# Rotary rows by DMA, and compressed blocks read with a stride

## The reference, cut to what matters

```
def partial_rope(x, pos):            # 16 of the 64 channels of each head are rotated
    ang = pos[:, None] * inv_freq    # 8 frequencies
    x1, x2 = x[..., :8], x[..., 8:16]
    rot = concat([x1 * cos - x2 * sin, x2 * cos + x1 * sin])
    return concat([rot, x[..., 16:]])

q_n   = partial_rope(q_b) ...        # 8 query heads of 64
k_cmp, k_slc, k_win = partial_rope(kc_b), partial_rope(ks_b), partial_rope(kw_b)

def compress_blocks(kv, pos_emb, w1, w2):       # kv: 256 tokens, 2 groups of 64 channels
    idx = arange(15)[:, None] * 16 + arange(32) # 15 overlapping blocks of 32 tokens
    blocks = kv[:, idx] + pos_emb[:, None, :]
    hid = silu(einsum('bnlgd,ldh->bgnh', blocks, w1))
    return einsum('bgnh,hd->bgnd', hid, w2)
```

## Time and profile before

| | |
|---|---|
| median of the runs | 890.04 us |
| profiled execution, its own time | 890.07 us |
| its span | 888.3 us |
| PE busy | 874.8 us (98%) |
| DVE busy | 586.1 us (66%) |
| ACT busy | 440.2 us (50%) |
| POOL busy | 51.3 us (6%) |
| DMA queue of SP | 150.44 MB |

### The profile page before, as it was taken

How to read it: one execution, slowest core, us unless ns; L and a number is a source line. 1 busy time by engine, 2 the same in 40 slices (tenths; PEclk the granted TensorE clock), 3 DMA queues, 4 the chain that set the end, 5 groups by cost and what they waited for, 6 DMA issues and landing times.

```text
span 888.3 us, 13795 instructions
## 1 busy us (share of the span) xinstructions
PE 874.8 (98%) x5624; PEld 759.6 (86%) x5624; DVE 586.1 (66%) x898; ACT 440.2 (50%) x644; POOL 51.3 (6%) x78
## 2 busy tenths in 40 slices
PE   8999999999999999999999999999999999999997
PEld 6888999898999888888889999877788888888885
DVE  5785664565656755555686997956477667777544
ACT  6644444753345544544485652466254555555442
POOL 1000000000020110000020015200000100000000
PEclk9999999999999999999999999999999999999999
DMA  9757644456454554556757683412555556665441
GB/s 294 239 190 227 223 144 142 143 166 183 127 184 153 184 179 153 175 183 198 263 145 248 159 174 95 144 49 49 143 190 181 180 184 190 189 190 190 166 166 48
DMA packets 127813, 151.67 MB, mean 171 GB/s; under 512 B 16983, under 2 KB 93142, under 8 KB 127750
## 3 DMA queue, kind: packets, MB, share of 16 engines
q1 hardware_dynamic: 127466, 150.44, 53.8%
q10 hardware_dynamic: 220, 0.28, 0.1%
q0 software_dynamic: 64, 0.07, 0.0%
HBM read 148.67 MB, written 3.68 MB: 172 GB/s over the span
## 4 chain that ended last, share of the span: by engine, by line
PE 87%; DVE 8%; ACT 2%; issue 1%; DMA 1%; POOL 0%; POOLq 0%; SPq 0%; ACTq 0%; DVEq 0%
PE bank L519 18%; PE bank L521 17%; PE bank L520 17%; PE bank L1357 9%; PE bank L546 5%; PE bank L1360 5%; PE bank L548 2%; DVE w_lo L2141 2%; DVE arena L2553 1%; PE bank L1017 1%; PE bank L751 1%; PE bank L731 1%; PE bank L850 1%; DMA arena<-in_x 1%; PE bank L711 0%
## 5 line engine op out<-in xcount | busy, mean ns | idle before, releaser
L2141 DVE TENSOR_TENSOR w_lo<-ring,w_hi 128x2048 fp32r<-128x2048 f32 (+1 forms) x134 | 297.5, 2230 | 120.4 <-ACT w_hi L1566 120.0
L1566 ACT ACTIVATE w_hi<-ring 128x2048 fp32r<-128x2048 f32 (+1 forms) x134 | 249.1, 1861 | 93.0 <-PE bank L521 71.5
L519 PE MATMUL bank<-h_both,w_hi 128*128 128x256 f32 x488 | 140.3, 287 | 0.4 <-DVE w_lo L2141 0.4
L520 PE MATMUL bank<-h_both,w_hi 128*128 128x256 f32 x488 | 138.0, 283 | 0.0
L521 PE MATMUL bank<-h_both,w_lo 128*128 128x256 f32 x488 | 138.0, 283 | 0.0
L1357 PE MATMUL bank<-h_both,w_hi 128*128 128x512 f32 x352 | 96.5, 395 | 0.8 <-DVE arena L2867 0.8
L519 PEld LDWEIGHTS bank<-h_both,w_hi 128*128 128x128 f32 x488 | 93.5, 192 | 2.4 <-issue 1.4
L520 PEld LDWEIGHTS bank<-h_both,w_hi 128*128 128x128 f32 x488 | 93.6, 192 | 0.1
L521 PEld LDWEIGHTS bank<-h_both,w_lo 128*128 128x128 f32 x488 | 93.5, 192 | 0.0
L519 PE MATMUL bank<-w_hi,h_both 128*128 128x512 f32 (+1 forms) x192 | 73.7, 384 | 0.0
L521 PE MATMUL bank<-w_hi,h_both 128*128 128x512 f32 (+1 forms) x192 | 71.5, 372 | 0.0
(11 more groups left out here) (387 smaller groups left out, 1525.9 us busy)
## 6 DMA issues: line engine op xcount, KB each, us to landing
ring<-in_w_in SPq DMA_DIRECT2D x59, 1024.0 KB, 5.1
ring<-in_w_gate_up SPq DMA_DIRECT2D x44, 512.0 KB, 4.7
ring<-in_w_down SPq DMA_DIRECT2D x10, 1024.0 KB, 5.0
ring<-in_w_mem_kv SPq DMA_DIRECT2D x8, 1024.0 KB, 10.0
ring<-in_w_gla_out SPq DMA_DIRECT2D x4, 1024.0 KB, 5.0
ring<-in_w_x_out SPq DMA_DIRECT2D x4, 1024.0 KB, 5.2
ring<-in_w_dsa_out SPq DMA_DIRECT2D x4, 1024.0 KB, 5.2
ring<-in_w_o SPq DMA_DIRECT2D x4, 1024.0 KB, 4.9
```

What stands on the lines that cost most here:

```text
L519: mm(o, ah, bh, start=start, stop=False, skip_group_check=True)
L520: mm(o, ah, bl, start=False, stop=False, skip_group_check=True)
L1566: act(w_hi[:, k % NHI, at:m], ring[:, order.index(name) % NSLOT, at:m], ACT.Copy)\
L2141: tt_(w_lo[:, i, at:m], ring[:, i, at:m], w_hi[:, k % NHI, at:m].bitcast(F), ALU.subtract)\
```

## The change

SP now moves the rotary rows. For each of the seven tiles 0, 1, 2 and 4 to 7, six DMAs inside the core's own memory collect the 16 rotary rows of both groups in a compact tile `rot` and once more, with the halves swapped, in `rot_turned` (`gather`, 42 DMAs). DVE does the rotation there with three instructions for each of two compact tiles (`rope`), the sign being in the table of sines. SP writes the rows back (`spread`, 14 DMAs). For the blocks of compressed tokens SP copies kc and vc into `blocks` (`block_rows`, 24 DMAs, of which 8 need the rotated rows); POOL writes the position rows beside them once; the 64 matmuls read their stationary operand with a stride of 16 tokens, and one matmul with a constant `pick` adds the partial rows and the position part. On PE the banks r0 to r3, sh0 and sh1 are gone, on POOL `rope_cos`, on DVE the sine products, the additions and the sixteen block additions. In the first block one small matmul (bank ik2) becomes a copy on ACT. SP's list of weight loads is not changed, but the DMAs stand in it:

```
             for i, name in enumerate(order):
                 s = i % NSLOT
+                if name == order[order.index("nq0") + NSLOT + 1]:
+                    sp.wait_ge(signal("roped"), 1)
+                    block_rows(0, 0, 16, lambda g: rot[16 * g:16 * g + 16, 0, :], "kc_blocks")
+                    spread(0)
                 if i >= NSLOT:
                     sp.wait_ge(*unit_used[order[i - NSLOT]])
+                    before = order[i - NSLOT]
+                    if before in ("kcks", "kwvc", "nq0", "nq1"):
+                        sp.wait_ge(*read(before))
+                    if before == "kcks":
+                        gather(0)
+                        gather(1)
+                        block_rows(0, 16, 64, lambda g: ns[64 * g + 16:64 * g + 64, 0, :], "kc_blocks")
+                    if before == "kwvc":
+                        gather(2)
+                        block_rows(1, 0, 64, lambda g: ns[64 * g:64 * g + 64, 3, :], "vc_blocks")
+                    if before == "nq0":
+                        gather(4)
+                        gather(5)
+                    if before == "nq1":
+                        gather(6)
+                        gather(7)
+                    if before == "vsvw":
+                        sp.wait_ge(signal("roped"), 2)
+                        spread(1)
```

```
+            def gather(tile):
+                i = int(tile > 4)
+                for g in range(2):
+                    at = 32 * rot_tiles[i].index(tile) + 16 * g
+                    sp.dma_start(rot[at:at + 16, i, :], ns[64 * g:64 * g + 16, tile, :]).then_inc(signal(f"gathered{i}"), 16)
+                    sp.dma_start(rot_turned[at:at + 8, i, :], ns[64 * g + 8:64 * g + 16, tile, :])\
+                      .then_inc(signal(f"gathered{i}"), 16)
+                    sp.dma_start(rot_turned[at + 8:at + 16, i, :], ns[64 * g:64 * g + 8, tile, :])\
+                      .then_inc(signal(f"gathered{i}"), 16)
+            def spread(i):
+                for a, tile in enumerate(rot_tiles[i]):
+                    for g in range(2):
+                        at = 32 * a + 16 * g
+                        sp.dma_start(ns[64 * g:64 * g + 16, tile, :], rot[at:at + 16, i, :])\
+                          .then_inc(signal(f"spread{i}"), 16)
+            def block_rows(kv, a, b, source, done):
+                for part, g, q in itertools.product(range(2), range(2), range(2)):
...
+                    sp.dma_start(blocks[kv][part][64 * q + a:64 * q + b, 256 * g:256 * g + n], source(g)[:, at:at + n])\
+                      .then_inc(signal(done), 16)
```

On PE:

```
             head_products("qg", 0)
-            pe.wait_ge(*read("kwvc"))
-            rope_turn("r0", 0, 2)
-            rope_turn("r1", 2, 1)
             project_channels("nq1", h_parts)
             head_transposes("kk", 4)
-            pe.wait_ge(*read("nq0"))
-            rope_turn("r2", 4, 2)
             pe.wait_ge(signal("silu_done"), 6)
             head_transposes("vt", 8)
-            pe.wait_ge(*read("nq1"))
-            rope_turn("r3", 6, 2)
-            pe.wait_ge(signal("rope_done"), 1)
-            for kv, tile in ((0, 0), (1, 3)):
-                bank = open_bank(f"sh{kv}")
...
             project_tokens("vsvw", h_parts)
             w = (plain_unit("w1k"), plain_unit("w1v"))
             bank = open_bank("hid")
-            for kv in range(2):
-                pe.wait_ge(*read(f"sh{kv}"))
+            pe.wait_ge(signal("positions"), 4)
+            pe.wait_ge(signal("vc_blocks"), 16 * 8)
+            pe.wait_ge(signal("kc_blocks"), 16 * 16)
...
-            pe.wait_ge(signal("rope_done"), 4)
+            pe.wait_ge(signal("spread0"), 16 * 8)
             level(1)
             hidden_sum()
             nsa_logits(0)
             nsa_logits(1)
             compressed_keys()
             level_end(1)
+            pe.wait_ge(signal("spread1"), 16 * 6)
             compressed_scores()
```

On DVE, whose scores also wait for both spreads, because they overwrite `rot`:

```
+            def rope(i):
+                n = rot_rows[i]
+                x, turned = rot[0:n, i, :], rot_turned[0:n, i, :]
+                ve.wait_ge(signal(f"gathered{i}"), 16 * 6 * len(rot_tiles[i]))
+                tt_(turned, turned, const("sin")[0:n, :], ALU.mult)
+                step(tt_(x, x, const("cos")[0:n, :], ALU.mult))
+                tt_(x, x, turned, ALU.add).then_inc(signal("roped"), 1)
...
-            lows(splits_by["r1"] + 1)
+            rope(0)
+            lows(splits_by["qg1"] + 1)
...
+            lows(ahead[0])
+            rope(1)
             ahead[0] = splits.index("z1") + 1
...
+            ve.wait_ge(signal("spread0"), 16 * 8)
+            ve.wait_ge(signal("spread1"), 16 * 6)
             for i in range(4):
                 nsa_scores(i)
```

More of the change, by code:

```diff
@@ L56, in _const_columns @@
     for name, width in (("ident", 128), ("diag3", 384), ("keep", S), ("chunk", 128), ("bucket", 383), ("pad", 1),
-                        ("lev", 6 * 64), ("id64", 64), ("chunk64", 64), ("after", 128), ("rope", 128), ("cos", S), ("sin", S), ("selg", 256),
-                        ("ones", 1),
+                        ("lev", 6 * 64), ("id64", 64), ("chunk64", 64), ("after", 128), ("cos", S), ("sin", S),
+                        ("pick", 64), ("ones", 1),
                         ("cneg", 2 * 16), ("cvis", 2 * 16)):
@@ L95, in shape_constants @@
     put("diag3", np.concatenate([diag, np.zeros((128, 128)), diag], 1))
-    rot = np.zeros((128, 128), np.float32)
-    cos = np.ones((128, S), np.float32)
-    sin = np.zeros((128, S), np.float32)
     freq = np.float32(500000.0) ** (-np.arange(8, dtype=np.float32) / np.float32(8))
     ang = (np.arange(S, dtype=np.float32)[:, None] * freq.astype(np.float32)[None, :]).astype(np.float32)
[L101 to L116, removed]
+    sign = np.where(np.arange(128) % 16 < 8, -1.0, 1.0).astype(np.float32)
+    put("cos", np.cos(ang).T[np.arange(128) % 8])
+    put("sin", np.sin(ang).T[np.arange(128) % 8] * sign[:, None])
+    pick = np.zeros((128, 64), np.float32)
+    for q in range(4):
+        for n in range(30):
+            pick[32 * q + n + n // 15, 30 * (q // 2) + n] = 1
+            pick[32 * q + 15, 30 * (q // 2) + n] = 1
+    put("pick", pick)
     put("ones", np.ones((128, 1)))
@@ L326, in build @@
         cblk_at = raw_at + 8 * S
-        cblk = [flat(cblk_at + 480 * i, 480).rearrange("p (j n) -> p j n", j=16) for i in range(2)]
+        blocks = [[flat(mb_at + 1024 * kv + 512 * part, 512) for part in range(2)] for kv in range(2)]
+        rot, rot_turned = tiled(prob_at, 2, S), tiled(prob_at + 512, 2, S)
+        rot_tiles, rot_rows = ((0, 1, 2, 4), (5, 6, 7)), (128, 96)
         hid, hid_rows = flat(cblk_at + 968, 64), flat(cblk_at, 128)
@@ L1058, in _ @@
                     kv, k = q // 2, j + q % 2
-                    ins = mm(bank[32 * q:32 * q + 32, 0:128], flat(cblk_at + 480 * kv + 30 * k, 32), w[kv][:, k, :],
+                    by_offset = blocks[kv][k // 8].rearrange("p (m s) -> p s m", s=16)
+                    ins = mm(bank[32 * q:32 * q + 32, 0:128], by_offset[:, 2 * (k % 8), :], w[kv][:, k, :],
                              start=j == 0, stop=j == 14, tile_position=(0, 32 * q), skip_group_check=True)
@@ L1066, in hidden_sum @@
                 bank = open_bank("hs")
-                by_branch = ident.rearrange("p (a b) -> p a b", a=2)
-                mm(bank[:, 0:60], hid_rows, by_branch[:, :, 0:30], start=True, stop=False)
-                done("hs", mm(bank[:, 0:60], hid_rows, by_branch[:, :, 32:62], start=False, stop=True))
+                done("hs", mm(bank[:, 0:60], hid_rows, const("pick")[:, 0:60], start=True, stop=True))
             z_weights = {}
@@ new lines, in spread @@
+            def spread(i):
[6 more added lines that the diff above has]
+                for part, g, q in itertools.product(range(2), range(2), range(2)):
+                    n = 240 if g == 0 or part == 1 else 256 - q
+                    if part == 1:
+                        n -= q
+                    at = 16 * part + q
+                    sp.dma_start(blocks[kv][part][64 * q + a:64 * q + b, 256 * g:256 * g + n], source(g)[:, at:at + n])\
+                      .then_inc(signal(done), 16)
@@ L1630, in _ @@
             sc.wait_ge(*full("small"))
+            act(ikT[0], bank_of("small")[64:128, 0:256], ACT.Copy)
             act(smallT, bank_of("small")[:, 0:256], ACT.Copy).then_inc(bank_reader("small"), 1)
@@ L2078, in _ @@
             nc.gpsimd.tensor_tensor(egc, egc, cv[:, 0:4, :], ALU.mult).then_inc(signal("q_decayed"), 1)
+            for kv in range(2):
+                for part in range(2):
+                    lots = blocks[kv][part].rearrange("p (m s) -> p m s", s=32)[:, 7 + 8 * (1 - part)::8, 16:32:2] \
+                        if part == 1 else blocks[kv][part][:, 240:256:2].unsqueeze(1)
+                    pos = cmp_pos[kv][:, 8 * part:8 * part + 8].unsqueeze(1).broadcast_to([128, 1 + part, 8])
+                    nc.gpsimd.tensor_copy(lots, pos).then_inc(signal("positions"), 1)
             gp.wait_ge(*read("ss"))
```

(9 more changed lines are left out.)

32 lines of the change are left out of this document (1 added, 31 removed).

## The result

The changed kernel takes 915.43 us (914.92 to 916.83, 6 runs) against 890.03 (889.73 to 890.46, 6 runs) of the kernel before: a ratio of 1.0286, 95% interval 1.0275 to 1.0296. It is slower, as forecast, but by 25.4 us and not by 4.9, and outside the range. The profiled execution took 914.92 us with a span of 913.1, 24.8 longer than before.

The account below looks back on a forecast made before the run. PE, busy 874.8 of 888.3 us, was taken as the bound, with SP's queue as second limit. Terms 4.6 - 0.3 - 0.4 + 1.0 = +4.9 on 890.07 gave 895.0 us, range 889 to 901.5.

Parts of the forecast that it names:

- What it puts into SP's queue: SP's weight loads: 74 small DMAs ahead of z1 at 0.41 us per issue delay z1, so hs starts 4.6 us later.
- Rotations and copies off PE, 4.9 us, and hid earlier: PE before hid: removing rotations and copies takes about 4.9 us off PE's path, so hid is reached at 551.
- rival 1: SP's queue: small copies cost much less than 0.3 us, z1 is issued as before, hs 5.0 us earlier: 884.4 us; chance 0.14.
- The other new waits end earlier: Waits for block rows and spreads: rotated block rows land at 549.4, spreads at 552.7 and near 563.7, before they are needed.
- hs released by ACT behind z1, with PE idle for 8 to 10 us: Sign in the profile after: PE idles 8 to 10 us in front of hs until ACT copies hid near 564.
- One matmul for hs and the lower clock, -0.3 and +1.0: PE from hs on: one matmul instead of two saves 0.3 us; the lower clock after idling costs 1.0 (0 to 5.75).
- rival 3: PE behind hs: lower clock holds the whole stretch, +5.75 instead of +1.0, 899.7 us; with longer issues 904; chance 0.15.
- The copy on ACT in place of a matmul in the first block, -0.4: First block: a PE matmul of 0.64 us becomes a copy on ACT, saving 0.4 us (0 to 0.6).

Follow-up runs that it names:

- experiment 1: Kernel before, with groups of eight small copies issued behind its end: SP took 0.63 us per copy inside the core, 0.45 with an end in device memory.
- experiment 5: Changed kernel with each SP weight load issued ahead of its slot's copies and z1 ahead of the gathers of nq0: 914.03 us, ratio 1.027.
- experiments 6 to 8: Changed kernel, its 80 copies divided over SP, POOL and ACT: loads first 895.31 us; then z0 and the next load held 892.64; then queue order mended, z0 unheld 890.6.

## Why the prediction was wrong

**The step that failed** is the issue term of "What it puts into SP's queue": "I take 0.41, the mean of the two with 16 rows, and keep 0.36 and 0.46". The queue took 0.68 per copy in the changed kernel, and experiment 1 has 0.63 on an idle chip. 74 x (0.68 - 0.41) = 20 us, and that is the miss: z1 left at 574.46 instead of the predicted 555.3, 19.2 us later. From there the working holds. z1 landed after 5.5 us (5.9 predicted), ACT split it and copied hid, and hs followed: +23.07 instead of +4.6.

The error under it was one of kind. The rows taken as neighbours all have one end in device memory, and experiment 1 gives 0.45 for those, too, so they had been read rightly. They were no bound for a copy with both ends in the core. The sentence in front of the number said that the trace has no such copy, but the interval was then made from the spread inside the other kind, 0.36 to 0.46, as if that covered the unknown. With 74 repeats each tenth of a microsecond is 7.4 us; the range ended 6.5 us above the forecast and could not hold an error of 0.27.

**The other terms.**
- Rotations and copies off PE, 4.9 us, and hid earlier: right in size. Without copies hid starts at 550.40 (551 predicted) and hs 6.1 earlier; rival 1 had 884.4 for that, and 884.06 was measured. So what it said PE would gain was right; its price for an issue (under 0.3) was off by more than the forecast's.
- "The other new waits end earlier": wrong, by the same term. PE waited 11.84 us in front of hid for the block copies. This cost nothing on top, because hs waited for z1 anyway; experiment 5 shows that it takes over the moment z1 is early.
- hs released by ACT behind z1, with PE idle for 8 to 10 us: right in kind, but it was 13.96.
- One matmul for hs and the lower clock, -0.3 and +1.0: together +1.8 measured, from hs to the compressed scores 5.56 us instead of 3.72. Windows of the profile after (the eighth figure is the granted clock):

```profile
575.00:580.00 5.00, 0.00 (x0) 0.00 (x0) 1.18 (x3) 0.00 (x0) 0.00 (x0) 0.50 0.74 221
580.00:586.00 6.00, 3.39 (x18) 2.54 (x18) 3.37 (x9) 3.33 (x6) 0.00 (x0) 0.50 0.72 242
586.00:588.00 2.00, 2.00 (x40) 1.68 (x40) 1.39 (x10) 0.94 (x5) 0.00 (x0) 0.68 1.05 391
588.00:592.00 4.00, 4.00 (x80) 3.58 (x74) 3.46 (x15) 3.26 (x15) 0.13 (x1) 1.00 0.67 244
```

  PE stood idle, the clock fell to its 1.2 GHz level, and the matmuls behind hs ran at it until about 587: the logits took 2.93 us instead of 1.58. The value taken near the lower end of 0 to 5.75 was about a microsecond too small; rival 3 was not what happened.
- The copy on ACT in place of a matmul in the first block, -0.4: nothing. ACT's copy of kcks starts at 519.59 in both traces.

Rival 1 also stood for a rule of the Trainium skill, "DMA: Bandwidth & Descriptors", section "Issuing engines are not separate DMA queues", that initiating a DMA is usually short beside the transfer. For these copies it is not: in experiment 1 ACT took 0.64 us to issue each, and each landed 1.8 us after its issue began, so a row of eight took 5.08 us to issue.

## What to carry to other kernels

Count the DMAs that a change puts in front of a weight load, by queue, and price them by a row of the same kind (both ends in the core or not): here 74 copies of 8 to 64 KB held SP's queue for 50.7 us, and the three loads of 1 MB among them for 3.5. Where no row has the kind, the bound is not the spread of another kind, and a term that is multiplied by 74 wants a measurement of its own. If such copies are needed, divide them over every queue that idles, and look for the wait that comes next: reordering the one queue gave back 1.4 us, dividing it 20, mending the order inside the queues 5 more.

## What the runs showed of the hardware

- On an idle chip a copy inside the core's memory takes SP 0.63 and ACT 0.64 us to issue, one to or from device memory takes SP 0.45; 8, 16 or 128 rows made little difference (5.35, 5.02 and 5.05 us for eight).
- POOL issues the same copy in 0.49 us, faster than SP or ACT.
- Such a copy landed 1.6 to 1.8 us after its issue alone. On the path of experiments 6 to 8 it landed 3.9 to 5.8 us after the start of the last issue in the six places named with a weight load in flight, and 1.7 to 1.8 in the two with none.
- The logits took PE 2.93 us at a granted clock of 0.50 (1.2 GHz), behind 13.96 us of idleness, and 1.58 us in the kernel before at 1.00.
